# Decoding in one stage by sequence in a one-core hybrid decoder step: heads times tokens as stationary rows, pages sorted ahead

## The chip, the cores and the metric

The kernel runs on one core of a Trainium2 chip. All data are float32. The metric is the device time of one launch in microseconds (us); the time before is the median of 3 runs.

## The reference, cut to what matters

One layer of a decoder with three groups of heads that work side by side, run for a prompt of 4096 tokens and for a decode batch of 8 sequences with 8 new tokens each. The change touches only the decode part. For each sequence it computes:

```python
# A: window attention, 6 query heads over 2 key heads, 1024 cached + 8 new keys
oa = mix_dilations([dilated_sample(aq, ka, va, d, w // d) for w, d in ((128,1), (512,4), (2048,16))])
# B: sparse attention: an indexer with 8 heads picks 256 of the 1032 keys per query
kb, vb, ki = (concat(pool[page_table], new) for pool, new in ...)   # 8 pages of 128 rows per sequence
dots  = einsum('nthd,nsd->ntsh', iq, ki)
score = einsum('ntsh,nth->nts', relu(dots), iw)                     # weighted sum over the 8 heads
sel   = top_k(where(causal, score, -inf), 256)
ob    = softmax(bq @ kb[sel]) @ vb[sel]                             # 6 query heads over 2 key heads
# C: cross attention, 4 heads, 256 memory tokens per sequence
oc = softmax(cq @ mk) @ mv
y  = x + [silu(ag)*oa | silu(bg)*ob | silu(cg)*oc] @ w_out, then RMSNorm
```

A head has 64 dimensions. The three dilation patterns are one attention with a bias per distance (the logarithm of how many patterns hold a key). The pages of a sequence lie scattered in a pool of 80 pages.

## The kernel before, in words

The program is a row of stages, each with its own tiles and a barrier at its end: `project_memory`, `project_tokens`, `attend_window`, `attend_sparse`, then `attend_sampled` twice ("b" with heads B, and "a" with heads A and C), then `project_out`. A stage can't load anything before the one ahead is over. Intermediate results pass between stages through scratch tensors in HBM.

`attend_sampled` has two parts. The first (lines 1910 to 2040) is a loop over the 8 sequences with one buffer: SyncE and ScalarE issue the loads of a sequence, TensorE turns (transposes) its key blocks, VectorE copies them from PSUM to `kT`. The next sequence's loads wait until the last one's keys are turned (line 1962). For "b" each page is looked up in a register (line 1923), and its rows are loaded with their own DMAs: 64 for the keys, 64 for the values, 128 for the indexer keys.

The second part is `attend` (lines 547 to 1012), a general attention over row tiles. It holds all 64 queries (8 sequences times 8 tokens) of one head as the stationary operand, and since each sequence has its own keys, it does one product per sequence, with a stationary operand `qm` that is zero in all columns but that sequence's 8 (`scores`, line 687: 8 products accumulate into one bank). The weighted values work in the same way: `PT` holds for each key block 8 copies, each zero but for one sequence, so that a block of 128 keys takes 8 products of 64 columns (`values`, line 705). Indexer scores come first (8 heads times 3 chunks of 512, 512 and 128 columns, times 8 sequences), then VectorE adds up relu(score) times weight (lines 877 and 881), then it searches the cut for 256 keys per row by 12 rounds of halving (`rounds`, line 904, each one compare-and-count over 1152 columns and two short operations), asks TensorE whether some row needs 12 more rounds (line 742), picks the exact value among the 8 largest below, and makes the bias. Then the 6 heads of B follow, and in the next stage the 4 heads of C and the 6 of A.

`attend_sparse` (from line 1300) does the same for the prompt: 32 query tiles t, with SyncE's program (lines 1461 to 1489) in order: constants, first keys and queries, and then for each t it waits, loads the queries of tile t+4 and t+2 and stores the result of tile t-1. The engines wait for the constants at lines 1545 and 1841.

A float32 product shows as two matmul records, a transpose as one.

Of the kernel before, what the change touches and what calls it, by code (L numbers as in the profile page):

```python
# [23 lines left out]
F32 = mybir.dt.float32  # L24
BF16 = mybir.dt.bfloat16
U16 = mybir.dt.uint16
I32 = mybir.dt.int32
# [441 lines left out]
class Tally:  # L469

    def __init__(self, sem, credit, per, tiles):
        self.sem, self.credit, self.per = sem, credit, per
        self.base = [credit + sum(p * n for p, n in zip(per[:g], tiles[:g])) for g in range(len(per))]

    def at(self, g, j, k):

        if isinstance(j, int):
            return self.base[g] + j * self.per[g] + k  # L480
        return j * self.per[g] + (self.base[g] + k)


class Attend:


    def __init__(self, kind, head, chunks):
        self.kind, self.head, self.chunks = kind, head, chunks
        if kind == "C":
            self.slot, self.half, self.out = T_CQ + head // 2, head % 2, (12 + head) * HD  # L490
        else:
            self.slot, self.half = (T_AQ if kind == "A" else T_BQ) + head % 3, head // 3
            self.out = (head if kind == "A" else 6 + head) * HD


def spans(lo, hi):
    return [(c, min(512, hi - c)) for c in range(lo, hi, 512)]


STAGES = 6  # L500


class Group:

    def __init__(self, tiles, idx, b_chunks, a_chunks, kinds):
        self.tiles, self.idx = tiles, idx
        self.width = sum(w for _, w in idx)  # L510
        order = (0, 3, 1, 4, 2, 5)
        self.heads = []
        if "B" in kinds:
            self.heads += [Attend("B", h, b_chunks) for h in order]
        self.n_b = len(self.heads)
        a_heads = [Attend("A", h, a_chunks) for h in order] if "A" in kinds else []
        c_heads = [Attend("C", h, [(0, MEM)]) for h in range(4)] if "C" in kinds else []

        self.heads += c_heads + a_heads
        self.n_idx = 8 * len(idx)  # L520
        self.first = [0]
        for a in self.heads:
            self.first.append(self.first[-1] + len(a.chunks))
        self.n_att = self.first[-1]
        self.s_all = self.n_idx + self.n_att

        self.n_a = max([self.first[i + 1] for i, a in enumerate(self.heads) if a.kind == "A"], default=0)
        self.s_b = self.n_idx + self.first[self.n_b]


        self.tail = max(self.n_b, len(self.heads) - STAGES)

    def part(self, a, lo, hi, n):

        at = lambda k: n * (self.first[k] - self.first[lo]) // (self.first[hi] - self.first[lo])
        return (at(a), at(a + 1)) if lo <= a < hi else (0, 0)

FEW_ROUNDS, ROUNDS = 12, 24
ASKED = 6 + 3 * FEW_ROUNDS + 4
MORE = 1 + 3 * (ROUNDS - FEW_ROUNDS) + 4
LINKS = ASKED + 2 + MORE + 14


def attend(nc, tag, R, nseq, groups, io):

    tiles = [g.tiles for g in groups]
    W = max([g.width for g in groups] + [512])
    WB = max([sum(w for _, w in a.chunks) for g in groups for a in g.heads if a.kind == "B"] + [W])
    SW = max(sum(w for _, w in a.chunks) for g in groups for a in g.heads)
    topk = any(a.kind == "B" for g in groups for a in g.heads)
    lastw = io["causal_width"]
    ptw = R if nseq == 1 else nseq * (R // nseq * (nseq + 1))  # L560
    with ExitStack() as ctx:
        def sb(name, shape, dt=F32):
            return ctx.enter_context(nc.sbuf_tensor(f"{tag}_{name}", shape, dt))

        def tally(name, credit, per):
            each = [per(g) for g in groups]
            used = any(each)
            return Tally(ctx.enter_context(nc.semaphore(f"{tag}_{name}")) if used else None, credit, each, tiles)

        io["open"](ctx, sb)  # L570
        ident, q_sb = io["ident"], io["q"]
        S = sb("S", [R, 2, SW])
        PT = sb("PT", [P, 2, 4, ptw])
        o_sb = sb("o", [R, D])
        mc = sb("mc", [R, 2, 8])
        mjunk = sb("mjunk", [R, 2, 8])
        negm = sb("negm", [R, 2])
        lsum = sb("lsum", [R, 2])
        linv = sb("linv", [R, 2])
        zero_bias = sb("zero_bias", [R, MEM])  # L580
        if topk:
            X = sb("X", [R, W])
            relu = sb("relu", [R, 4, 512])
            Y = sb("Y", [R, W])
            GE = Y[:, :].bitcast(BF16)[:, 0:W]
            GT = Y[:, :].bitcast(BF16)[:, W:2 * W]
            rank = sb("rank", [R, W], U16)
            biasB = sb("biasB", [R, WB], BF16)
            col = sb("col", [R, 24])
            undone = sb("undone", [1, 1], I32)  # L590
# [41 lines left out]
        def wait(eng, t, g, j, k):  # L632
            eng.wait_ge(t.sem, t.at(g, j, k))
# [1789 lines left out]
```

## Time and profile before

| | us |
|---|---|
| median of 3 runs (range) | 7368.91 (7368.54 to 7378.87) |
| the profiled execution's own time | 7375.32 |
| its span, first to last instruction | 7373.6 |
| stage "b" of the decode, first SyncE issue to that of "a" | 6026.81 to 6512.15 |
| stage "a", to the first issue of `project_out` | 6512.15 to 6794.17 |

Over the whole span TensorE is busy for 85%, VectorE for 49%, ScalarE for 38%. Read these as an average over seven stages with different limits; the stages of the decode are read by their own stretches.

### The profile page before, as it was taken

How to read it: one execution, taken by the hardware profiler on the slowest of the kernel's cores; microseconds unless marked ns; L12 is line 12 of the kernel's file. 1: busy time of each engine (PE TensorE's matmuls, PEld its weight loads, DVE VectorE, ACT ScalarE, POOL GpSimd, SP SyncE). 2: the span in 40 equal slices, each digit the busy share in tenths (PEclk: the TensorE clock that was granted, in tenths of full speed). 3: DMA queues.
4: the chain of work that ended last, by engine and by line, in shares of the span. 5: the costliest groups of instructions: out<-in, count | busy, mean ns of one | idle time of the engine just before them, and what ended most of it. 6: DMA issues, size and time to landing. Idle time of an engine off the chain costs nothing. (4 is left out here: it accounts for less than half of the span.)

```text
span 7373.6 us, 83535 instructions
## 1 busy us (share of the span) xinstructions
PE 6301.1 (85%) x27915; PEld 3737.0 (51%) x27915; DVE 3636.7 (49%) x9459; ACT 2834.3 (38%) x5992; POOL 113.6 (2%) x179
## 2 busy tenths in 40 slices
PE   6999999998999867888888888888888864858898
PEld 3444444445667634555555555555555642445444
DVE  1111111113555568888877777776776611210554
ACT  1222222223545534555555555555555520000232
POOL 0000000000000100000000000000000000000000
PEclk8999999999999978999999999999999977979999
DMA  3111111115000030000000000000000011021443
GB/s 116 51 44 47 49 51 48 42 45 140 30 26 34 29 85 16 16 11 11 11 11 6 6 11 6 6 6 6 6 7 1 4 26 48 1 74 49 141 150 129
DMA packets 261720, 294.02 MB, mean 40 GB/s; under 512 B 57700, under 2 KB 226660, under 8 KB 260196
## 3 DMA queue, kind: packets, MB, share of 16 engines
q1 hardware_dynamic: 226196, 240.36, 10.3%
q0 software_dynamic: 12368, 40.71, 1.5%
q10 hardware_dynamic: 22784, 8.40, 0.4%
q8 instruction: 184, 3.01, 0.2%
q14 instruction: 188, 1.54, 0.1%
HBM read 181.88 MB, written 109.60 MB: 40 GB/s over the span
## 5 line engine op out<-in xcount | busy, mean ns | idle before, releaser
L453 PE MATMUL t_zp<-t_w,t_xT 128*128 128x512 f32 (+1 forms) x3696 | 1443.1, 551 | 42.5 <-DVE t_w L406 42.5
L1514 PE MATMUL p_SC<-p_ikT,p_iq 128*128 128x512 f32 (+3 forms) x2272 | 1119.0, 599 | 217.2 <-DVE p_mc L1654 216.9
L1541 PEld LDWEIGHTS p_OP<-p_bv,p_PT 128*128 128x128 f32 x6336 | 877.6, 202 | 587.9 <-ACT p_PT L1580 284.6
L453 PEld LDWEIGHTS t_zp<-t_w,t_xT 128*128 128x128 f32 x3696 | 662.5, 192 | 778.3 <-issue 735.5
L1589 ACT ACTIVATE p_relu<-p_SC 128x512 f32<-128x512 f32 (+3 forms) x1136 | 633.5, 565 | 1076.1 <-PE p_SC L1514 954.6
L1541 PE MATMUL p_OP<-p_bv,p_PT 128*128 128x64 f32 x6336 | 872.8, 282 | 148.8 <-ACT p_PT L1580 148.6
L1505 PE MATMUL p_SC<-p_bkT,p_bq 128*128 128x512 f32 (+3 forms) x1728 | 884.9, 595 | 32.0 <-DVE p_mc L1654 31.8
L1514 PEld LDWEIGHTS p_SC<-p_ikT,p_iq 128*128 128x128 f32 x2272 | 440.6, 202 | 783.2 <-issue 422.8
L1654 DVE CUSTOM_DVE_ANT_0 p_S<-p_SC,p_bias 128x512 f32<-128x512 f32 (+3 forms) x864 | 554.5, 645 | 407.4 <-PE p_SC L1505 335.8
L1687 DVE SCALAR_TENSOR_TENSOR p_X<-p_relu,p_iw,p_X 128x1024 f32<-128x1024 f32 (+7 forms) x546 | 608.4, 1114 | 220.0 <-ACT p_relu L1589 213.1
L1580 ACT ACTIVATE p_PT<-p_TP 128x512 f32<-128x512 f32 (+3 forms) x864 | 481.4, 557 | 445.7 <-PE p_TP L1531 444.4
L288 ACT ACTIVATE t_z<-t_zp,t_rstd 128x512 f32<-128x512 f32 (+1 forms) x231 | 146.7, 635 | 1310.9 <-PE t_zp L453 1310.9
L1531 PE MATMUL p_TP<-p_ident,p_S 128*128 128x128 f32 x3168 | 533.1, 290 | 103.1 <-ACT p_S L1572 102.5
L1721 DVE TENSOR_SCALAR_CACHE_REDUCE p_Y<-p_X,p_col 128x384 bf16<-128x384 f32 (+29 forms) x240 | 609.6, 2540 | 1.0 <-issue 0.3
L1256 ACT ACTIVATE w_S<-w_S,w_o 128x256 f32<-128x256 f32 (+1 forms) x704 | 339.0, 482 | 416.0 <-DVE w_o L1222 416.0
L1572 ACT ACTIVATE p_S<-p_S,p_negm 128x1024 f32<-128x1024 f32 (+7 forms) x480 | 476.3, 992 | 16.8 <-DVE p_mjunk L1660 16.8
L1531 PEld LDWEIGHTS p_TP<-p_ident,p_S 128*128 128x128 f32 x3168 | 406.7, 164 | 126.0 <-ACT p_S L1572 120.5
L2305 PE MATMUL f_zp<-f_w,f_mixT 128*128 128x512 f32 x1056 | 463.9, 598 | 0.0
L1231 DVE COPY w_PT<-w_TP 128x512 f32<-128x512 f32 (+1 forms) x352 | 226.7, 644 | 263.3 <-PE w_TP L1166 263.0
L1184 PEld LDWEIGHTS w_OP<-w_v,w_PT 128*128 128x128 f32 x2052 | 250.6, 191 | 158.5 <-DVE w_PT L1231 158.5
L2305 PEld LDWEIGHTS f_zp<-f_w,f_mixT 128*128 128x128 f32 x1056 | 200.8, 193 | 240.6 <-issue 240.6
L1184 PE MATMUL w_OP<-w_v,w_PT 128*128 128x64 f32 x2052 | 290.1, 282 | 21.2 <-DVE w_PT L1231 20.7
(247 smaller groups left out, 5559.5 us busy)
## 6 DMA issues: line engine op xcount, KB each, us to landing
scr_qkT<-t_qT SPq DMA_DIRECT2D x33, 960.0 KB, 3.7
scr_part<-w_o POOLq DMA_DIRECT2D x96, 198.0 KB, 2.2
f_part<-scr_part SPq DMA_DIRECT2D x32, 594.0 KB, 4.8
t_x<-in_x_prompt SPq DMA_DIRECT2D x32, 512.0 KB, 3.6
f_gate<-scr_gate SPq DMA_DIRECT2D x32, 512.0 KB, 7.2
f_x<-in_x_prompt SPq DMA_DIRECT2D x32, 512.0 KB, 3.7
out_y_p<-f_y POOLq DMA_DIRECT2D x32, 512.0 KB, 6.5
p_iq<-scr_qkT SPq DMA_DIRECT2D x120, 128.0 KB, 2.9
```

The costliest lines, as they stand in the source:

```text
L453: mm = pe.matmul(zp[(NZ * p + c) % 2][:, 0:n], xT[:, p, k, :], w[:, k, a:a + n], start=(k == 0), stop=(k == KD - 1))
L1184: mm = pe.matmul(OP[u % 2][:, h, :], PT[:, k % 2, 2 * b + s, :], val, start=(b == U.blocks[0]), stop=(b == 1))
L1505: pe.matmul(bank(ring["B", n, g])[:, 0:w], bq[:, t % 2, n % HEADS, :], bkT[:, 512 * g:512 * g + w], start=True, stop=True).then_inc(s_read ...
L1514: pe.matmul(bank(ring["I", t, k])[:, 0:w], iq[:, t % 2, h, :], ikT[:, 512 * c:512 * c + w], start=True, stop=True).then_inc(s_ready, 1)
L1531: mm = pe.transpose(TP[m % 2][:, b, :], S[:, n % 3, c0:c0 + P], ident[:, :])
L1541: mm = pe.matmul(OP[n % 2][:, 0:HD], PT[:, m % 2, b, :], bv[:, 4 * g + b, s * HD:(s + 1) * HD], start=(g == 0 and b == 0), stop=(last and ...
L1580: act.activation(PT[:, m % 2, 0:nb, :], TP[m % 2][:, 0:nb, :], ACT.Copy).then_inc(pT_ready, 1)
L1589: act.activation(relu[:, j % 3, 512 * (c % 2):512 * (c % 2) + w], SC[r % 4][:, 0:w], ACT.Relu, scale=0.5)\
L1654: dve.tensor_tensor_reduce(S[:, n % 3, cols], SC[r % 4][:, 0:w], bias[:, cols], -SCALE, -FAR, ALU.add, ALU.min, mc[:, p, g:g + 1]).then_in ...
L1687: dve.scalar_tensor_tensor(x, r, w, x, ALU.mult, ALU.add).then_inc(idx_added, 1)
L1721: link(dve.tensor_scalar(G[:, 0:L], X[:, t % 2, 0:L], c(W + 1), None, ALU.is_gt, ALU.add, accum_out=c(CNT)))
L2305: mm = pe.matmul(zp[2 * p + i][:, :], mixT[:, p, k * P:(k + 1) * P], w[:, k, i * 512:(i + 1) * 512], start=(k == 0), stop=(k == KD - 1))
```

## The change

The two decode stages and `attend` with its helpers go; one new `attend_sampled` takes their place. It has these parts:

- **Pages.** `attend_sparse` now also copies the pages of all sequences in order into scratch tensors, HBM to HBM, with SyncE's DMAs: 24 per tile t for t = 4 to 11. It loads the page table with its constants (one more DMA before the first keys).
- **Keys.** A sequence's keys, values and indexer keys are loaded with one DMA each, 8 consecutive rows per partition, so that key order in `kT` is "partition within block" (host tables `window_s` and the bias follow that order). Keys and values of A and B share the tiles `kn` and `v`, with room for all 8 sequences.
- **Indexer.** Per sequence: 8 turns, then one product each for 512, 512 and 8 keys, with 8 heads times 8 tokens as the 64 stationary columns; relu on ScalarE; then 3 products with `pick_w` (the indexer weights, laid out so that they add up the heads of each token) that accumulate over the sequences in 3 banks.
- **Attention.** 24 units: C, A and B for each of 8 sequences. The stationary operand has 48 columns (6 heads times 8 tokens; half of each column zero, by key head) or 32 for C. The bias is added by a product with a selection matrix `sel` (for B it reads `bias` in steps of 8 elements). Values are one product per key block, 128 columns wide (256 for C), computed for both key heads. Scores stay in PSUM; ScalarE's exp reads them there.
- **Search.** 24 rounds always, 2 after each of units 1 to 12, over 1032 columns; the ends of the search after units 13, 14 and 15. The check on TensorE goes.
- **Output.** 16 small DMAs (6 heads of A, 6 of B, 4 of C).

The diff, cut to its core:

```diff
@@ attend_sparse
+            def sort_pages(n):
+                for b in range(PAGES):
+                    page = sp.value_load(table[0:1, n * PAGES + b:n * PAGES + b + 1], min_val=0, ...)
+                    for name, to in (("cache_idx_k", "page_i"), ("cache_dsa_k", "page_k"), ("cache_dsa_v", "page_v")):
+                        sp.dma_start(scr[to][n * PAST + b * PAGE:n * PAST + (b + 1) * PAGE, :],
+                                     ins[name][bass.ds(page * PAGE, PAGE), :]).then_inc(const_in, 16)
+            sp.dma_start(table[:, :], ins["page_table"]).then_inc(const_in, 16)
             keys(0)
...
                 if t:
                     store(t - 1)
+                if 4 <= t < 4 + NSEQ:
+                    sp.wait_ge(const_in, 128)
+                    sort_pages(t - 4)
...
@@ attend_sampled (new), SyncE
+            sp.dma_start(ident[:, :], ins["ident"]).then_inc(idx_in, 16)
+            for s in range(2):
+                sp.dma_start(iq[:, s:8:2, :], new_slots(slice(s * HD, (s + 1) * HD), T_IQ, T_AQ)).then_inc(idx_in, 16)
...
+            for h in range(8):
+                sp.dma_start(iw[h * TDEC:(h + 1) * TDEC, :], scr["iw"][SEQ:SEQ + R, h:h + 1]...).then_inc(idx_in, 16)
+            for n in range(NSEQ):
+                sp.dma_start(ikn[:, n, :, :], by_partition(scr["page_i"], n, PAGES)).then_inc(i_in[n], 16)
...
+            for n in range(NSEQ):
+                u = units.index(("A", n))
+                sp.wait_ge(turned, turn_at["K", u, 1] + 1)
+                sp.dma_start(kn[:, n, :, :], by_partition(scr["page_k"], n, PAGES)).then_inc(k_in[n], 16)
+                sp.wait_ge(v_done, u + 1)
+                sp.dma_start(v[:, n, :, :], by_partition(scr["page_v"], n, PAGES)).then_inc(v_in[n], 16)
+            for kind, done in (("C", 8), ("A", 16), ("B", 24)):
+                sp.wait_ge(o_out, done)
+                for head in range(4 if kind == "C" else 6):
+                    store(kind, TDEC * head, HD * (head if kind == "C" else head // 3), head)
@@ TensorE
+            def index(n):
...
+                    pe.matmul(score_bank(("I", n, c))[0:R, 0:w], iqn[:, n, :], keys, start=True, stop=True)
+            def sum_heads(n):
...
+                    pe.matmul(OP[c][0:R, 0:w], pick_w[:, n, :], relu[:, n % 2, a:a + w],
+                              start=(n == 0), stop=(n == NSEQ - 1)).then_inc(i_summed, 1)
+            def scores(u):
...
+                if kind == "B":
+                    pe.wait_ge(bias_ready, 1)
+                for c, (a, w) in enumerate(chunks(u)):
...
+                    to = score_bank((u, c))[0:rows, 0:w]
+                    pe.matmul(to, (qa if kind == "A" else qb)[:, n, :], keys, start=True, stop=False)
...
+                        add = bias[:, 0:PAST].rearrange("q (p b) -> q b p", b=PAGES)[:, 4 * c:4 * c + 4, :]
+                        to = to.rearrange("q (b p) -> q b p", p=P)
+                    pe.matmul(to, sel[:, n, :], add, start=False, stop=True).then_inc(s_ready, 1)
...
+            for n in range(NSEQ + 1):
+                if n < NSEQ: turn_index(n)
+                if n >= 1: index(n - 1)
+                if n >= 2: sum_heads(n - 2)
...
+            for u in range(NU + 2):
+                if u + 1 < NU: turn_keys(u + 1)
+                if u < NU: scores(u)
+                if 1 <= u <= NU: turn_probs(u - 1)
+                if u >= 2: values(u - 2)
@@ VectorE
+            for u in range(NU + 1):
+                if u + 1 < NU: keys(u + 1)
+                if u < NU: maxima(u)
+                if u >= 1: inverse(u - 1)
+                part(u)
@@ build
-    attend_sampled(nc, ins, outs, scr, "b", "B")
-    attend_sampled(nc, ins, outs, scr, "a", "AC")
+    attend_sampled(nc, ins, outs, scr)
```

The scores have 3 banks in turn (`score_bank` waits for the relu or exp that read the bank 3 uses ago), the turns have 2 (`turn_bank`).

## Rows read from the trace of the kernel before

**Rows 1.** Windows by stretch: us, busy us (instructions) per engine, clock, DMA share, GB/s.
```profile
6053.00:6196.00 143.00, 28.99 (x128) 26.00 (x128) 22.04 (x32) 0.00 (x0) 2.13 (x2) 0.55 0.30 77
6196.00:6324.00 128.00, 125.84 (x383) 49.44 (x384) 13.71 (x23) 11.36 (x23) 2.06 (x1) 0.98 0.00 1
6324.00:6368.00 44.00, 14.80 (x32) 4.53 (x31) 39.47 (x83) 0.27 (x1) 0.00 (x0) 0.65 0.00 0
6368.00:6509.00 141.00, 138.75 (x1179) 88.05 (x1178) 11.55 (x54) 13.80 (x35) 0.00 (x0) 1.00 0.00 1
...
6527.00:6610.00 83.00, 22.51 (x96) 19.38 (x96) 16.60 (x24) 0.00 (x0) 3.80 (x2) 0.54 0.48 136
6610.00:6791.00 181.00, 175.99 (x1406) 109.77 (x1406) 14.23 (x74) 18.13 (x52) 0.39 (x1) 0.99 0.00 1
```
**Rows 2.** Timeline (start us, us, what) at both ends of the decode.
```profile
6026.81 0.34 SPq L1976 DMA_DIRECT2D bk_ident<-in_ident  x1
...
6790.84 0.31 ACT L805 ACTIVATE a_o<-a_OP,a_linv 64x64 f32<-64x64 f32 x1 [4.33 <-PE a_OP L717]
...
6794.17 0.36 SPq L2125 DMA_DIRECT2D f_ident<-in_ident  x1
```
**Rows 3.** Groups by shape, TensorE, decode stages: busy us, mean ns.
```profile
L689 PE MATMUL b_SC<-bk_kT,bk_qm 128*64 128x512 f32 x448 | 198.9, 604 | 6.7 <-POOL b_PT L659 6.7
L717 PE MATMUL a_OP<-ak_v,a_PT 128*64 128x64 f32 x992 | 61.0, 222 | 4.3 <-ACT a_PT L794 4.3
L689 PE MATMUL a_SC<-ak_kT,ak_qm 128*64 128x128 f32 x96 | 11.5, 273 | 0.0
```
**Rows 4.** Timeline and chain, TensorE runs without a gap.
```profile
6628.97 3.62 PE L689 MATMUL a_SC<-ak_kT,ak_qm 128*64 128x256 f32 x16
...
7332.26 0.87 PE f_tp L2294 x8
7333.14 27.48 PE f_zp L2305 x64
```
**Rows 5.** Timeline, `attend_window`: keys read in steps (first), side by side (second).
```profile
1989.45 1.28 PE L1155 MATMUL w_SC<-w_akT,w_aq 64*128 64x256 f32 x4
...
2450.97 0.70 PE L1155 MATMUL w_SC<-w_ckT,w_cq 64*128 64x256 f32 x4
```
**Rows 6.** Groups by shape, VectorE and ScalarE, decode stages.
```profile
L2039 DVE COPY bk_kT<-bk_tr 128x512 f32 x32 | 22.0, 691 | 128.3 <-PE bk_tr L2015 127.0
L843 DVE CUSTOM_DVE_ANT_0 a_S<-a_SC,ak_biasA 64x512 f32<-64x512 f32 x12 | 8.2, 683 | 120.2 <-PE a_SC L689 120.2
L843 DVE CUSTOM_DVE_ANT_0 a_S<-a_SC,a_zero_bias 64x256 f32<-64x256 f32 x4 | 1.7, 416 | 26.1 <-PE a_SC L689 23.4 <-issue 2.7
L966 DVE TENSOR_TENSOR_SCAN b_rank<-b_Y 64x1152 uint16<-64x1152 bf16 x1 | 2.5, 2550 | 0.0
L848 DVE TENSOR_SCALAR_CACHE_REDUCE a_mjunk<-a_mc 64x3 f32<-64x3 f32 x6 | 0.9, 148 | 0.2
```
**Rows 7.** Timeline, VectorE: one round of the search and the next one's start.
```profile
6328.91 1.41 DVE L907 TENSOR_SCALAR_CACHE_REDUCE b_Y<-b_X,b_col 64x1152 bf16<-64x1152 f32 x1
...
6330.78 1.40 DVE L907 TENSOR_SCALAR_CACHE_REDUCE b_Y<-b_X,b_col 64x1152 bf16<-64x1152 f32 x1
```
**Rows 8.** DMA issues by line: count, KB each, median us to landing.
```profile
p_iq<-scr_qkT SPq DMA_DIRECT2D x120, 128.0 KB, 2.9
...
ak_nat<-in_cache_mem_k ACTq DMA_DIRECT2D x8, 256.0 KB, 4.4
```
**Rows 9.** Timeline of SyncE's issues in `attend_sparse`: one slow issue, tile 4, tile 12.
```profile
2582.91 6.49 SPq L1454 DMA_DIRECT2D p_bv<-out_dsa_v  x1
...
2798.60 2.60 SPq L1436 DMA_DIRECT2D p_iq<-scr_qkT  x4
2801.24 0.60 SPq L1439 DMA_DIRECT2D p_iw<-scr_iw  x1
...
3356.18 3.20 SPq L1436 DMA_DIRECT2D p_iq<-scr_qkT  x4
```

More of the change, by code:

```diff
@@ L466, in _ @@
             turn_z(NLAST, 0)
[L469 to L493, printed above, removed]
@@ L496, in spans @@
[L496 to L536, printed above, removed]
@@ L1857, in _, with attend_sampled, chunks, key_turns @@
                         all_seen()
-def attend_sampled(nc, ins, outs, scr, tag, kinds):
-    R, KEYS = NDEC, PAST + P
-    NB = KEYS // P
-    paged = kinds == "B"
-    keys = spans(0, KEYS)
-    groups = [Group(1, keys, [], [], ""), Group(1, [], keys, [], "B")] if paged else [Group(1, [], [], keys, kinds)]
-    DIAG = NSEQ * (R // NSEQ * (NSEQ + 1))
+def attend_sampled(nc, ins, outs, scr):
+    R, NEW = NDEC, PAST
+    KEYS = PAST + TDEC
+    L = KEYS
+    ROWS = {"A": 48, "B": 48, "C": 32}
+    units = [(kind, n) for kind in "CAB" for n in range(NSEQ)]
+    NU = len(units)
+    def chunks(u):
+        return [(0, 512), (512, 512), (NEW, TDEC)] if units[u][0] != "C" else [(0, MEM)]
+    def key_turns(u):
+        return 2 if units[u][0] != "C" else 1
+    first_chunk, first_turn = [0], [0]
+    for u in range(NU):
+        first_chunk.append(first_chunk[-1] + len(chunks(u)))
+        first_turn.append(first_turn[-1] + key_turns(u))
+    turn_at, turn_users, score_at, score_users = {}, [], {}, []
+    def plan_turn(name, user):
+        turn_at[name] = len(turn_users)
+        turn_users.append(user)
+    def plan_score(name, user):
+        score_at[name] = len(score_users)
+        score_users.append(user)
+    def plan_key_turns(u):
+        for i in range(key_turns(u)):
+            plan_turn(("K", u, i), ("keys", 2 * NSEQ + first_turn[u] + i + 1))
+    for n in range(NSEQ + 1):
+        if n < NSEQ:
+            for i in range(2):
+                plan_turn(("I", n, i), ("keys", 2 * n + i + 1))
+        if n >= 1:
+            for c in range(3):
+                plan_score(("I", n - 1, c), ("relu", 3 * (n - 1) + c + 1))
+    plan_key_turns(0)
+    for u in range(NU + 2):
+        if u + 1 < NU:
+            plan_key_turns(u + 1)
+        if u < NU:
+            for c in range(len(chunks(u))):
+                plan_score((u, c), ("exp", first_chunk[u] + c + 1))
+        if 1 <= u <= NU:
+            plan_turn(("P", u - 1), ("probs", u))
```

932 lines of the change are left out of this document (370 added, 562 removed).

## The prediction

> **What bounds the kernel now.** I read the windows first, stretch by stretch, since shares over the whole span mix seven stages. They show the decode in four kinds of stretch [rows 1]: two loops that load and turn keys, where TensorE is busy for 28.99 of 143 us and 22.51 of 83 us; two stretches of scores and values where it is busy nearly all the time (138.75 of 141 us, 175.99 of 181 us) at full clock; the indexer, 125.84 of 128 us; and the search, where VectorE is busy for 39.47 of 44 us and TensorE mostly waits. Nothing of these lies beside another. The timeline gives the ends: first issue at 6026.81 us, first issue of the output stage at 6794.17 us [rows 2]. So the decode costs **767.4 us**, a tenth of the span, and it is all path. The groups by shape say why the full stretches are long: 448 records of 512 columns for 64 stationary columns, 56 of which are zero, and 992 records of 64 columns for values [rows 3]. Eight products do what one could.
>
> **Prices.** One 512-column record takes 27.48 / 64 = 0.429 us in an unbroken run, a turn of 128 columns 0.87 / 8 = 0.109, a 256-column record 3.62 / 16 = 0.226 [rows 4]; a record of 128 columns 11.5 / 96 = 0.120, one of 64 columns 61.0 / 992 = 0.0615 [rows 3]. A float32 product is two records. The new products differ in height and stationary width (48 instead of 64), not in what moves through, so I use these.
>
> **Head of the new stage.** SyncE issues 13 DMAs before the first indexer keys: 5 at about 0.4 to 0.6 us and 8 small ones, 7 us at 0.60 each for the latter [rows 9]. Then 256 KB land in 4.4 us [rows 8]. The eight DMAs for the weights move single elements; I give them the same landing. TensorE starts 11.5 us in; no memset stands ahead of it. Bounds 9 and 20.
>
> **Indexer.** Per sequence 8 turns (0.87), 8 records of 512 columns (3.43), 4 of 8 columns (at most 0.25): 4.55 us, times 8 is 36.4. VectorE's two copies (2 x 0.69 [rows 6]) and ScalarE's relus, about as long, lie beside it, since the program turns one sequence ahead and sums one behind. TensorE comes out of a pause at the lower of its two clock levels: the load loops ran at 0.55 [rows 1]. With that and the last relu and sum: 3.5 us more. Then VectorE takes the three sums from PSUM and copies the first keys while TensorE waits: 3 us.
>
> **C units: VectorE sets the pace.** TensorE needs 4 turns (0.44), 4 records of 256 columns for scores and 4 for values (0.226 each, 1.81) and 2 small turns (0.22): 2.5 us. VectorE needs a copy (0.69), a maximum over 256 columns (0.42, the row of that size), three short operations with their read-outs (0.6, from 0.148 each [rows 6]), 0.2 for links, and two rounds. A round is 6330.78 - 6328.91 = 1.87 us [rows 7]; its long operation shrinks from 1152 to 1032 columns, 1.41 x 0.104 = 0.15 less: 1.72, two are 3.45. Together 5.35 us, times 8 is 43 us. This is where the search goes: before it stood alone.
>
> **A units: nearly level.** TensorE: 8 turns 0.87, scores 8 records of 512 (3.43) and 4 tiny ones (0.25), 9 turns of the probabilities at no more than 0.109 (0.98), 18 value records of 128 columns (2.16): 7.7 us, times 8 is 61.5. VectorE: two copies 1.38, two maxima at 0.68 [rows 6], a small one, short operations 0.9, two rounds 3.45: 7.2 us. So TensorE leads by 0.5 us in the first five. The last three units carry the ends of the search. The old stretch of the search is 44 us, less 12 x 1.87 leaves 21.6 for setting up, the question to TensorE, and the ends [rows 1, 7], among them a scan of 2.55 us [rows 6]; I put the ends at 15 us, 5 each, 1.6 over two rounds. Less the slack and plus the wait of the first B unit for its bias: 4 us. The bank ring also makes each unit's scores wait for the last one's exp: maximum, negation, exp, about 2.3 us from 0.68, 0.148 and an exp of a chunk; between them TensorE has probabilities, values and the next turns, 4.0 us, to do. Hidden, as long as VectorE answers at once.
>
> **B units.** The same 7.7 us, but the bias product reads every 8th element. The window stage shows such a read: four records of 256 columns with keys in steps take 1.28 us, against 0.70 side by side [rows 5], twice the time once the end of the run is taken off. Of the four records pairs run beside each other there, so the ratio is what carries over: four bias records of 0.429 gain between 0 (if only the queries' steps cost) and 1.72 us. I take 1.6: 9.3 us, times 8 is 74.4. VectorE (3.7) lies beside.
>
> **Clock, against the rule.** In the search TensorE was busy for 14.80 of 44 us and was granted 0.65; in dense stretches 0.98 to 1.00 [rows 1]. C units have it busy for 2.5 of 5.35 us, so I expect a clock below 1. At 1.2 GHz its 2.5 become 4.9 us, still under VectorE's 5.35: nothing lost. The first A unit can pay up to 7.7 us; I take 2. The Trainium skill (TensorE: Matmul & The Clock Gate, "HAM oscillation — how this bites in real kernels") says that a loop whose products are shorter than its waits starts each turn at half rate; by that rule the loss would return in every C unit, and the sum would be the same, since VectorE covers it.
>
> **Tail.** After the last values one output, six stores at about 0.5 us, of which the last lands 2 us later, and the next stage; before, the same way took 6794.17 - 6790.84 = 3.3 us [rows 2]. With the last wait for the exp: 6.5 us. The stores of C and A go out earlier.
>
> **Loads.** 7 MB must be in before the first A unit, 97 us into the stage, at 136 GB/s 51 us; all of A is 14 MB, 103 us, and the last A unit comes at 150 [rows 1]. B's loads of sequence n go out during A's unit n, 60 us ahead. Hidden. If the rate were 70 GB/s, A's units would wait some 50 us.
>
> **Sorting.** 24 issues and 8 look-ups in each of 8 tiles. At 0.60 us an issue [rows 9] and up to 1 us a look-up, 22 us. Tiles 4 to 11 last 3356.18 - 2798.60 = 557.6 us, 70 each, of which SyncE used 5. Behind the copies in SyncE's order stand the queries of two tiles ahead and the store of a tile with two buffers; both have more slack than 22 us. Traffic of 20 MB in 558 us is 36 GB/s beside nearly nothing. I take 0, bounds -1 and +30. The table's DMA ahead of the first keys delays the sparse stage by 0.6 to 1 us: 1.
>
> **Sum.** 11.5 + 36.4 + 3.5 + 3 + 43 + 61.5 + 4 + 2 + 74.4 + 6.5 = 246 us in place of 767.4: 521 less, plus 1. From the profiled execution's 7375.3 us that gives 6855. It stands 6.4 us over the median, so the **prediction is 6848 us**.
>
> **Rivals.** (1) *The two engines wait for each other in turn* (0.30). VectorE's margin in A is 0.5 us, the turns have 2 banks and the scores 3, so a late copy stops TensorE and then a late score stops VectorE. With A at 10, B at 10.5 and C at 6.5 us a unit this costs 18 + 10 + 9 = 37 us: 6885. For it speaks that maxima read PSUM in an order fixed by the program; against it the old stages, where TensorE's waits for the other two engines were small. (2) *Steps cost nothing and the seams are short* (0.15): the bias read is as fast as a plain one (-13) and head and tail are 5 us shorter: 6830. Against it stands the row of the window stage. (3) *The sorting goes wrong and eats it all* (0.02): slower than before. An issue that meets a full queue took 6.49 us [rows 9]. Of the 558 us of the eight tiles some 512 are free for SyncE, and the gain is 521, so it needs (512 + 521) / 192 = 5.4 us for each copy before the kernel is slower. At 6.49 the eight tiles take 1246 + 46 us in place of 558, and the kernel 6848 + 734 = 7580. Against it: between the tiles the queue is empty, and issues there take 0.60. (4) *The small DMAs or the loads hold the stage* (0.08): single-element DMAs landing at 20 us, or 70 GB/s: 6875 to 6900. The forecast itself has 0.45.
>
> **Numbers.** A difference under 0.2% (15 us) can't be told from none. The likeliest case's own range is 6832 to 6866; with rivals 1 and 2 the range is 6822 to 6895. Faster than before by over 0.2%: 0.97; within 0.2%: 0.01; slower: 0.02.
>
> **What would show it.** Right: one decode stage of some 246 us; C units spaced by 5 to 6 us with VectorE busy all along and a clock under 1; A units spaced by 7.7 and B units by 9 to 9.5 with TensorE busy; bias records of B twice as long as those of A; tiles 4 to 11 of the sparse stage as long as before. Wrong: A units spaced by over 8.5 us with both engines idle in part; B as short as A; a first turn later than 20 us; TensorE waiting for `kn` or `v`; the sparse stage longer by more than 5 us.

## The result, and the profile after

The changed kernel takes 6868.76 us (median of 4 runs, 6855.58 to 6893.19); the kernel before 7370.95 (median of 4, 7368.54 to 7378.87). The ratio is 0.932, with a 95% interval of 0.929 to 0.935. The forecast was 6848, the range 6822 to 6895. Two things want explaining: a median 21 us above the forecast, and runs 38 us apart where those of before lie within 10.

The profiled execution took 6855.58 us, the forecast's 6855 for that execution. That the two agree to a microsecond is luck: the decode took 4.6 us more than forecast, and all the rest of this execution (6605.0 us, before 6608.0) 4.0 us less than the 6609.0 that the forecast implies. Windows of the changed kernel, in the columns of [rows 1]: the sparse stage, then the decode in five stretches (head, indexer, C units, A units with the first B unit, B units; the limits lie near the changes from one kind of unit to the next, not on them).

```profile
2573.00:6017.00 3444.00, 2922.75 (x13588) 1865.75 (x13588) 2521.71 (x6135) 1841.62 (x3392) 1.59 (x2) 0.93 0.05 15
6017.00:6028.00 11.00, 2.39 (x11) 1.68 (x12) 2.18 (x4) 0.00 (x0) 3.01 (x5) 0.50 0.52 149
6028.00:6072.00 44.00, 41.68 (x173) 18.67 (x171) 15.89 (x34) 10.50 (x26) 0.00 (x0) 0.97 0.91 323
6072.00:6120.00 48.00, 35.37 (x130) 14.49 (x130) 42.42 (x133) 9.03 (x35) 0.00 (x0) 0.86 0.04 12
6120.00:6189.00 69.00, 65.32 (x356) 34.83 (x356) 49.30 (x135) 19.50 (x64) 0.00 (x0) 0.93 0.28 92
6189.00:6264.00 75.00, 74.31 (x358) 34.63 (x358) 20.52 (x71) 18.33 (x59) 0.00 (x0) 0.98 0.08 24
```

Before, three stretches had TensorE busy for a fifth to a third of the time, beside VectorE or beside transfers alone. Now TensorE is busy nearly all along behind the head (2.39 of 11 us), and the one stretch where it isn't (35.37 of 48 us) is VectorE's (42.42). The loads for the C and A units fall under the indexer, at 323 GB/s, so the 70 GB/s at which the A units would have waited was never near.

The timeline gives the ends, as in [rows 2]:

```profile
6016.79 0.34 SPq L1451 DMA_DIRECT2D d_ident<-in_ident  x1
...
6263.73 2.02 SPq L1448 DMA_DIRECT2D scr_o<-d_oB  x6
6267.39 0.36 SPq L1874 DMA_DIRECT2D f_ident<-in_ident  x1
```

The decode lasts 6267.39 - 6016.79 = **250.6 us** (before 767.4, forecast 246). Each unit leaves one output copy on ScalarE, and the starts of these copies give the spacing of the units: mostly 5.0 us for C (the first six copies lie 4.97 to 5.89 us apart), 8.12 for A, 10.03 for B.

TensorE in the steady B unit, and its waits over the decode:

```profile
6198.94 1.06 PE L1558 MATMUL d_SC<-d_kT,d_qb 128*48 128x512 f32 x2
6199.93 2.01 PE L1566 MATMUL d_SC<-d_bias,d_sel 64*48 64x512 f32 x2
6201.87 1.06 PE L1558 MATMUL d_SC<-d_kT,d_qb 128*48 128x512 f32 x2
6202.86 2.01 PE L1566 MATMUL d_SC<-d_bias,d_sel 64*48 64x512 f32 x2
```

```profile
PE d_TR L1509 <- DMA d_ikn<-scr_page_i: 11.6, 1, 11.6
PE d_TR L1537 <- DVE d_kT L1694: 9.6, 6, 3.1
PE d_SC L1558 <- DVE d_bias L1782: 3.0, 1, 3.0
```

From start to start the stepped bias pair takes 6201.87 - 6199.93 = 1.94 us, the pair of queries and keys 0.99. The waits (total us, times, longest) are the head, the copies in the C units, and one of 3.0 us for the bias ahead of the first B unit. In the steady A units there are none: between 6130 and 6165 us TensorE was busy for 35.00 of 35.

Outside the decode: the sparse stage runs from 2573.32 to 6016.79, 3443.5 us (before 3448.5). The output stage takes 586.4 us in place of 579.4; over the twelve traces with the new decode it lay between 583.5 and 592.4, and it took 585.6 in `one`, which has the decode stages of before. So the change needn't be the cause of these 7 us; their cause is open. The stages differ from trace to trace without any edit of theirs: the sparse stage with the sorting in it took between 3439.9 and 3457.2 us in eleven traces.

### The profile page after: what moved, and what is told of

It is laid out like the page before. It is cut to its first block and busy times, and to the rows that moved or that the text cites. A ratio compares the mean times of both kernels' runs of the same rounds, so it can differ in the third digit from the quotient of the medians.

```text
span 6853.8 us, 78452 instructions
## 1 busy us (share of the span) xinstructions
PE 6011.2 (88%) x25717; PEld 3541.6 (52%) x25717; DVE 3647.1 (53%) x9535; ACT 2846.6 (42%) x6063; POOL 91.9 (1%) x172
## 5 line engine op out<-in xcount | busy, mean ns | idle before, releaser
L638 PEld LDWEIGHTS w_OP<-w_v,w_PT 128*128 128x128 f32 x2052 | 250.6, 191 | 158.6 <-DVE w_PT L685 158.6
L386 DVE COPY t_qT<-t_tp 128x512 f32<-128x512 f32 (+1 forms) x132 | 81.4, 654 | 447.7 <-PE t_tp L439 446.6
```

## Experiments

Decode lengths below run from the stage's first DMA issue to that of the output stage, in the one profiled execution of each run. All but `late` and `one` have the sorting in the sparse stage. `late`, `one` and `rounds12` were executed once; the times of the others are of 4 or 5 executions.

**same** and **same2**: the changed kernel, unedited.

> The changed kernel itself, once more, to see what its spread of 38 us over four runs (6855.58 to 6893.19, against 10 us of the kernel before) is made of, and as the base of its neighbours in this job. Theory 'the spread lies in the long stages' (they are 6603 of 6854 us and have granted TensorE clocks of 0.91 to 0.99): the decode stage repeats within 2 us at 250.6, A units at 8.12 and B units at 10.03 us apart, the first B unit again near 16 us; differences lie in the projections, the sparse stage or the output stage, and go with their clock. Rival 'the new stage is unstable' (its engines wait for each other in turn, and the seam before the first B unit falls differently each time): the decode stage itself differs by over 10 us from 250.6.

> The changed kernel once more, beside the kernel with full products ahead of the indexer on one chip: the runs so far of the two were on different chips (4 for the latter, whose five runs lie within 5.7 us; 9 and another for the changed kernel, 38 and 43 us apart). Theory 'the indexer's clock stays low in some runs, and full products ahead of it prevent that': this kernel again has two groups of runs 34 us apart (two or three of six at 6885 to 6901), the other none. Rival 'it is the chip that differs': both kernels agree in their spread here.

`same`: 6858.08, 6862.28, 6895.10 and 6900.71; the decode of the profiled one 250.6 us, every spacing as before to 0.02 us. `same2`, on another chip: 6891.52 to 6901.45, all five, with a decode of 284.2 us. The 13 times of this kernel (4 of the result, 4 and 5 here) form two groups: five from 6855.6 to 6872.5, and eight from 6891.5 to 6901.5. Three of the 13 were profiled, two of the lower group and one of the higher. TensorE in one sequence of the indexer, in `same2`, and the window around it:

```profile
6059.47 3.67 PE L1518 MATMUL d_SC<-d_kT,d_iqn 64*64 64x512 f32 x4
...
6063.12 3.77 PE L1524 MATMUL d_OP<-d_relu,d_pick_w 64*64 64x512 f32 x6
6066.82 1.91 PE L1509 MATMUL d_TR<-d_ident,d_ikn 128*64 128x128 f32 x8
6068.66 3.67 PE L1518 MATMUL d_SC<-d_kT,d_iqn 64*64 64x512 f32 x4
```

```profile
6036.00:6056.00 20.00, 20.00 (x43) 7.51 (x42) 3.04 (x5) 3.73 (x9) 0.00 (x0) 0.50 1.07 340
6056.00:6076.00 20.00, 20.00 (x44) 7.53 (x42) 2.73 (x4) 2.49 (x6) 0.00 (x0) 0.50 0.83 333
6076.00:6096.00 20.00, 20.00 (x43) 7.50 (x43) 3.91 (x12) 2.49 (x6) 0.00 (x0) 0.50 0.00 0
```

and the same place in the first profile of the changed kernel:

```profile
6037.46 1.93 PE L1518 MATMUL d_SC<-d_kT,d_iqn 64*64 64x512 f32 x4
...
6039.31 1.97 PE L1524 MATMUL d_OP<-d_relu,d_pick_w 64*64 64x512 f32 x6
6041.22 1.06 PE L1509 MATMUL d_TR<-d_ident,d_ikn 128*64 128x128 f32 x8
6042.21 1.93 PE L1518 MATMUL d_SC<-d_kT,d_iqn 64*64 64x512 f32 x4
```

A sequence takes 9.19 us (6059.47 to 6068.66) instead of 4.75, with a granted clock of 0.50, the level of 1.2 GHz, from end to end although TensorE is busy every microsecond. The instructions are the same. The DMA share goes from 1.07 to 0.00 with no effect, so it isn't the loads. Both theories of `same` are half wrong: the stage is stable by unit, but the gap between the groups lies in it, in one place (284.2 - 250.6 = 33.6 us). Of the eight traces in which this indexer runs with nothing put ahead of it and its height unchanged, three (`after`, `same`, `early`) show it at 1.00 and five (`same2`, `plain`, `tall`, `rounds12`, `late`) at 0.50. That the unprofiled times of the higher group have the same cause is a conclusion from the times and from the clock of the whole execution, which is 0.939 to 0.942 in that group and 0.945 to 0.947 in the other.

**warm**: full products ahead of the indexer; **warm2**: the same beside `same2`.

```diff
+            pool.memset(warm[:, :], 1.0).then_inc(zeroed, 1)
...
+            pe.wait_ge(zeroed, 1)
+            for k in range(5):
+                pe.matmul(OP[2][:, :], warm[:, 0:P], warm[:, :], start=True, stop=True)
             pe.wait_ge(idx_in, IDX_IN)
```

> Five float32 products of 128 rows x 128 columns x 512 columns, on a tile of ones and into a bank that is written anew later, on TensorE while it would wait for the first indexer keys. The result is the same. Of six traces of kernels with this indexer, four show it at full clock (35 us at 1.00, first turn to first turn of the compressed units 40 us) and two at 0.50 from end to end (74.3 us), with the same instructions and TensorE busy all along; both the kernel's fast and its slow runs lie 34 us apart for that. Theory 'the products of 64 rows and 64 columns can't bring the clock up by themselves, but keep it': with full products ahead of them all runs have the indexer at 1.00, the high group of runs (6893 to 6901) is gone, the spread falls from 38 us to that of the kernel before (10 us), the median is 6855 to 6860 and the head of the stage is 0 to 2 us longer or shorter. Rival 'the low level is independent of what ran just before' (chance of the chip): 1 to 3 of 6 runs are still 34 us longer.

> The kernel with five full products ahead of the indexer once more, on the chip of its neighbour. Theory: all runs within 10 us of each other and of 6861. Rival 'it is the chip': its runs spread as its neighbour's do; with one run above 6885 the theory that the products prevent the low level falls.

(The first of these miscounts, and so does that of `high` below: until then three traces had shown the full clock and two the low one, and 3 of 8 times of the unedited kernel had been above 6885.) `warm`: 6861.57 (6859.23 to 6864.90, 5 runs). `warm2`: 6862.99 (6859.49 to 6870.74, 5 runs) where `same2`, on the same chip, has 6894.37. Ratios to before are 0.9315 (0.9302 to 0.9327) for `warm2` and 0.9358 (0.9345 to 0.9371) for `same2`. So five products whose result nobody uses save 31 us on that chip, and it isn't the chip that differs. Windows of `warm`:

```profile
6024.00:6028.00 4.00, 4.00 (x7) 1.58 (x6) 0.31 (x1) 0.00 (x0) 0.34 (x2) 0.59 0.34 56
6028.00:6036.00 8.00, 7.08 (x36) 3.50 (x35) 4.55 (x8) 1.49 (x4) 0.00 (x0) 1.00 1.06 306
6036.00:6060.00 24.00, 24.00 (x102) 10.97 (x101) 7.00 (x15) 6.39 (x16) 0.00 (x0) 1.00 1.04 361
```

The added products run from 6021.11 to 6028.7 us; the clock rises under them and stays up through the small ones. No run has five small products in their place, so that they must be full ones is not shown.

**high**: 128 rows for the indexer's scores.

```diff
-iqn = sb("iqn", [HD, NSEQ, R])
+iqn = sb("iqn", [P, NSEQ, R])      # rows 64 to 127 zero, as in kT
-  kT[0:HD, n % 2, 512 * c:512 * c + 512]
+  kT[:, n % 2, 512 * c:512 * c + 512]
```

> The indexer's scores (32 of its 48 long records and more, not its sums over heads) get 128 rows in place of 64, the lower half zeros; nothing is added ahead. The result is the same and the number of records too. Theory 'how much of the array a product uses decides whether the clock rises': no run with the indexer at 0.50, or fewer than before (2 of 6 traces, 4 of 9 times of the unchanged kernel above 6885), the median near 6858. In turn the switch of height in each sequence (128-row scores, 64-row sums) costs, by the 0.13 us seen in the A units, 2 x 0.13 us a sequence, 2 us in all. Rival 'only the number of records or the time busy counts': as many runs at 6893 as without, median 6875.

6866.90 (6863.67 to 6873.14, 5 runs), none in the group above 6885, no product added, decode 250.6 us. The edit gives 128 rows to 32 of the indexer's 64 long records (not of 48, as the expectation has it). With twice the rows under the same 64 columns the profiled run has the indexer at 1.00, and the other four times leave no room for 34 us more. The indexer itself, first turn to last sum, is 1.3 us longer than in `same`, where 2 were expected for the changes of height. That speaks for the theory, and against the rival; but only five runs on one chip stand behind it, and the unedited kernel was not run on that chip. The one run there with the old indexer in its old form is `late`, whose trace has it at 0.50.

**plain**: the bias put into key order once.

```diff
-    add = bias[:, 0:PAST].rearrange("q (p b) -> q b p", b=PAGES)[:, 4*c:4*c+4, :]
+    add = biasp[:, a:a + w]
...
-    link(dve.tensor_scalar(bias[:, :], bias[:, :], 1.0, -NEG, ...))
+    dve.tensor_scalar(biasp[:, 0:PAST].rearrange("q (b p) -> q p b", p=P),
+                      bias[:, 0:PAST].rearrange("q (p b) -> q p b", b=PAGES), 1.0, -NEG, ...)
```

> The bias of the B units is put into key order once, by the last VectorE operation of the search, and read side by side by TensorE. Theory 'the stepped read costs all that B is longer than A' (my term of 1.6 us a unit; the record takes 1093 ns for two where the window's takes 608): B units fall from 10.03 to 8.1 us apart, 8 x 1.9 = 15 us less, the decode stage at 236 to 238 us, less what a stepped VectorE operation over 1024 columns costs in front of the first B unit (1.07 us for 512 columns against 0.69, so about 1 us more). Rival 'B is longer for another reason' (its product with the queries, the values, or the clock after the seam): B stays above 9.5 us and the bias records keep their 1.0 us.

B units are 8.12 us apart, the same as A's. The bias pair in `plain`, 0.99 us from start to start:

```profile
6257.66 1.06 PE L1564 MATMUL d_SC<-d_biasp,d_sel 64*48 64x512 f32 x2
6258.65 1.06 PE L1559 MATMUL d_SC<-d_kT,d_qb 128*48 128x512 f32 x2
```

The read in steps was the whole difference, 1.91 us a unit, as the first theory has it. The decode took 271.9 us with the indexer at the low clock; less the 33.6 by which `same2` is longer than `same`, 238.3, an estimate. Its median, 6880.93 (6873.12 to 6894.40), can't show 12 us beside a clock that is worth 34.

**tall**: selector, window and bias with 128 rows.

```diff
-sel = sb("sel", [R, NSEQ, 48])
+sel = sb("sel", [P, NSEQ, 48])     # and window, bias; rows 64 to 127 zero
```

> The selector, the window and the bias get 128 rows instead of 64, with zeros in the lower half, so that all products of the A and B scores have the same height. The result is the same. An A unit takes 8.12 us and not the 7.7 that I summed, with TensorE busy all along; between a product of 128 rows and one of 64 the starts of two 512-column records lie 0.99 us apart, where 0.86 was expected; the indexer, where all have 64 rows, keeps 0.44 each. Theory 'changing the height costs some 0.13 us at each change': pairs return to 0.86 us, an A unit to 7.6 us (four pairs a unit, 0.5 us less), 8 x 0.5 = 4 us off A; in B, where the stepped record is 1.94 us a pair, up to as much again, 4 to 8 us in all. Rival 'the pair costs 0.99 whatever the height' (alternating weights, or two accumulations into one bank): no unit moves by over 0.1 us.

A units are 7.51 us apart, B units 9.47. An A unit in the first profile of the changed kernel, then the same place in `tall`:

```profile
6164.74 1.06 PE L1558 MATMUL d_SC<-d_kT,d_qa 128*48 128x512 f32 x2
6165.73 1.06 PE L1566 MATMUL d_SC<-d_window,d_sel 64*48 64x512 f32 x2
6166.72 1.06 PE L1558 MATMUL d_SC<-d_kT,d_qa 128*48 128x512 f32 x2
```

```profile
6170.95 1.02 PE L1569 MATMUL d_SC<-d_window,d_sel 128*48 128x512 f32 x2
6171.80 1.02 PE L1561 MATMUL d_SC<-d_kT,d_qa 128*48 128x512 f32 x2
6172.66 1.02 PE L1569 MATMUL d_SC<-d_window,d_sel 128*48 128x512 f32 x2
```

The pair is back at 0.86 us; each change between 128 and 64 rows had cost 0.13. More zeros to multiply, less time. The decode is 272.7 us, 239.1 after taking off the low clock's 33.6: some 11.5 less, where 4 to 8 were expected; 2 of it lie at the first B unit, where the clock's fall is shorter here (3.4 us in place of 10.2). The median, 6878.80 (6842.39 to 6891.94), shows this no better than that of `plain`.

**early**: the ends of the search one unit sooner.

```diff
-                elif u <= 12:
-                    rounds(2 * u - 2, 2 * u)
-                elif u < 16:
-                    (mask_above, pick_value, make_bias)[u - 13]()
+                elif u <= 11:
+                    extra = max(0, min(2, u - 8))
+                    rounds(2 * u - 2 + max(0, min(2, u - 9)), 2 * u + extra)
+                elif u < 15:
+                    (mask_above, pick_value, make_bias)[u - 12]()
```

> The last four of the 24 rounds are done two at a time earlier (three rounds instead of two in the units 9 and 10), and the three ends of the search one unit sooner, so that the bias is ready a unit before TensorE wants it. Now the first B unit waits 3.02 us for it, after which the granted clock is 0.54 and the unit takes 16.05 us instead of 10.03. Theory 'the wait brings the clock down, and the clock costs the other 3 us': both go, the first B unit takes 10 to 10.5 us, the decode stage is 6 us shorter (244.6), less up to 0.3 us in each of the two units with three rounds, where VectorE (28 of 35 us busy) then needs 8.3 us. Rival 'the clock falls for another reason at that place' (the stepped bias, or chance): the 3 us of waiting go, but the unit still takes 13 us and the granted clock is under 0.8. Second rival 'three rounds overrun': units 9 and 10 take over 9 us and give back what the seam saves.

The wait for the bias is gone, and the first B unit takes 11.45 us in place of 16.05; the decode is 247.3 us, 3.3 less. The clock still falls, but later and for a shorter time (3.4 us in place of 10.2). Windows of `early` around the first B unit:

```profile
6174.00:6178.00 4.00, 3.77 (x12) 0.77 (x9) 1.38 (x2) 0.66 (x2) 0.00 (x0) 1.00 0.83 265
6178.00:6182.00 4.00, 4.00 (x18) 1.36 (x17) 1.55 (x6) 0.00 (x0) 0.00 (x0) 0.94 0.00 1
6182.00:6186.00 4.00, 4.00 (x24) 3.60 (x23) 0.30 (x5) 2.37 (x8) 0.00 (x0) 0.63 0.00 0
```

So the 3 us of waiting are not the clock's only reason; neither theory holds alone. The two A units with three rounds take 8.34 us, 0.2 more, and the last interval before the first B unit takes 8.74, 0.6 more; so 4.6 us saved become 3.3. The median, 6890.16 (6851.01 to 6894.10), has four of five runs in the group of the low clock and can't show them.

**rounds12**: one round a unit, `rounds(u - 1, u)`; the output is another.

> The search does one round a unit in place of two, so 12 of its 24 rounds are left out and the selected keys may be others. Theory 'VectorE sets the pace of the compressed units and TensorE that of the A units': the C units, now 5.02 us apart, come 1.72 us closer (3.3 to 3.5 us), or down to 4.9 us only where TensorE is then at its lower clock level; the A units stay at 8.12 us to 0.05. In all 12 to 14 us off the stage at full clock. Rival 'the engines wait for each other in turn': the A units get shorter too, by 0.3 us or more, since 28 of 35 us on VectorE become 19.

C units, by the output copies on ScalarE:

```profile
6126.51 0.45 ACT L1655 ACTIVATE d_oC<-d_OP,d_linv 32x256 f32<-32x256 f32 x1
6129.81 0.45 ACT L1655 ACTIVATE d_oC<-d_OP,d_linv 32x256 f32<-32x256 f32 x1
6133.10 0.45 ACT L1655 ACTIVATE d_oC<-d_OP,d_linv 32x256 f32<-32x256 f32 x1
```

3.30 us apart, one round (1.72) less than 5.02, and the A units stay at 8.12. VectorE sets the pace of the one, TensorE of the other; the engines don't wait for each other in turn. The decode is 274.2 us with the indexer at the low clock, 10.0 less than in `same2` and not the expected 12 to 14: the first B unit, with its fall of the clock, takes 1.1 us more than there, and one B unit 1.6 more.

**late**: the sorting at the head of the decode stage, the loop over `sort_pages(n)` moved out of the sparse stage and waited for.

> The sorting of the pages into scratch is moved from the sparse stage to the head of the decode stage, where nothing covers it: the page numbers are fetched, 8 x 24 copies issued, and the first load waits for the last of them. The work is the same. Theory 'the sorting is hidden in the sparse stage, and what it costs in the open is SyncE's issue time': blocks of three copies 2.57 us apart, 64 of them, 165 us, plus the fetch and the last landing (3 + 3 us): decode stage 250.6 + 171 = 421 us, the sparse stage as long as now (3443.5 us), time 7027. Rival 'in the open the copies are bound by their own traffic' (20 MB read and written): at the 140 GB/s of the first loads it takes 143 us for reading alone, 286 us for both ways, and the time is 7140; the issues then meet full queues. Second rival 'the sorting costs the sparse stage something now': it gets shorter by more than 3 us.

SyncE in `late`, the first copies, the last block, and what comes behind it:

```profile
6019.73 0.59 SPq L1446 DMA_DIRECT2D scr_page_i<-in_cache_idx_k  x1
...
6022.43 0.49 SPq L1446 DMA_DIRECT2D scr_page_i<-in_cache_idx_k  x1
...
6184.90 0.53 SPq L1446 DMA_DIRECT2D scr_page_v<-in_cache_dsa_v  x1
6187.11 0.36 SPq L1454 DMA_DIRECT2D d_ident<-in_ident  x1
```

The sorting takes 6187.11 - 6017.48 = 169.6 us in the open, at 2.6 us for a block of three (64 of them from 6019.73 to 6185.43). The sparse stage without it lasts 3443.65 us in this trace, with it 3443.5 in the first profile. That these two agree within 0.2 us is chance, since the same stage with the sorting differs by 17 us from trace to trace. The eight tiles alone are a narrower measure: from the issue of `p_iw` in tile 4 to that in tile 12 they take 553.4 to 560.3 us in the eleven traces with the sorting, and 554.2, 558.2 and 558.3 in the three without it (`late`, the kernel before, `one`). So a piece of work worth 170 us, a third of the gain, costs nothing that can be seen beside a variation of 7 us. The second rival's 3 us can't be told apart from this variation. The decode is 203 us longer than 250.6: the 170, and 34 for the indexer, which ran at the low clock in this profile; the time is 7064.41 us, the forecast 7027 plus these 34 and 3 more. The traffic of 20 MB held nothing up (the DMA share was 0.24 during the sorting), so the first rival falls.

**one**: the kernel before, `range(1)` for `range(nseq)` in its score and value loops.

> The kernel before, with the products of one sequence in place of all eight in its score and value loops of the decode (7/8 of these products are left out, the output of the decode is another). It splits the gain of 517 us. By the groups of before, 448 + 96 score records at 0.44 and 0.12 and 992 value records at 0.0615 are 272 us of start-to-start time, of which 7/8 go: 233 to 238 us. Theory 'TensorE bounds the full stretches (138.75 of 141 and 175.99 of 181 us)': the decode falls from 767.4 to 530 us, and the other 280 us of the change's gain come from doing loads, turns, search and attention beside each other. Rival 'behind TensorE another engine is close': the stretches are left with the copies, maxima and exps of VectorE and ScalarE (11.55 and 13.80 of 141 us, so not close) or with waits from one to the other, and the decode stays above 580 us.

7046.02 us, the decode 433.9: 333.5 less than before. My expectation was wrong in its input: it took three groups of the decode's products and there are more (192 further records of 512 columns, 864 further of values). All of them, at the prices of the prediction, are 640 x 0.429 + 64 x 0.226 + 320 x 0.12 + 1856 x 0.0615 = 442 us, 7/8 of that 386. Of the 53 us that didn't come, TensorE's group of long score records in `one` shows 34.9 as waits for VectorE, behind the search; what holds the other 18 is open (the group, then the window over the old indexer with 125.84 of 128 us in [rows 1], now with the search in it):

```profile
L689 PE MATMUL b_SC<-bk_kT,bk_qm 128*64 128x512 f32 x56 | 32.4, 719 | 41.6 <-DVE b_mc L843 34.9 <-POOL b_PT L659 6.7
```

```profile
6196.00:6324.00 128.00, 49.38 (x248) 24.57 (x246) 86.86 (x215) 24.94 (x60) 6.72 (x4) 0.66 0.02 5
```

So of 517 us some 333 come with not multiplying by zeros. The other 184 are what the rest of the change brings on top of it: the overlap of loads, turns, search and attention, one stage in place of two, fewer DMAs, pages sorted ahead. No run separates these. `one` is a single execution, and another order of the two steps could share the 517 us differently.

**best2**: plain, tall, early and warm together.

> The four edits together: bias in key order (B units 10.03 to 8.12 us apart, stage 12.8 us shorter when the indexer runs at full clock), selector, window and bias of 128 rows (A units 8.12 to 7.51, the stage 12 us shorter), the ends of the search a unit earlier (3.3 us shorter), and the full products ahead of the indexer. If they add up: A and B units both 7.5 us apart, the stage 250.6 - 12.8 - 12 - 3.3 = 222.5 us, less 2 to 3 because with both of the first two the B unit saves its height switch twice over or not at all (its bias pair was 1.94 and becomes 0.86). The time 6827 us with the indexer at full clock, and always there by the first theory of the run with products ahead; 6861 in a third of the runs by its rival. A rival for the sum: with A units of 7.5 us VectorE (28 of 35 us in five units of 7, or 7 us a unit, and 8.7 with three rounds) becomes the bound, and the units with three rounds take 8.7: 2.4 us back.

6834.40 us (6827.35 to 6840.69, 5 runs), ratio to before 0.928 (0.926 to 0.929), beside `warm` at 6861.57 on the same chip; the forecast was 6827. The decode is 221.5 us, the forecast 222.5 less 2 to 3. B units are 7.51 us apart, and so are the A units that VectorE doesn't hold up. The granted clock of the B units is 1.00 (this window goes to the end of the stage, so the tail's idle 4 us are in it):

```profile
6180.00:6246.00 66.00, 61.91 (x404) 39.65 (x402) 22.78 (x79) 20.07 (x67) 0.00 (x0) 1.00 0.13 38
```

The first B unit takes 7.49 us, with no fall of the clock. VectorE now does hold three of the A units (8.35, 8.35 and 9.44 us), as the rival for the sum has it for the first two; the third is the one beside the last end of the search, which no theory had.

## Why the prediction was right, and where it was off

The gain of the decode, 517 us of the 521 forecast, came by the way that the prediction describes: one product for eight, the search beside C and A units, the sorting under the sparse stage. The sizes below are mostly a few microseconds off, in both directions.

In the order of its sum, cut at events of the trace (first turn, end of the indexer, starts of the output copies), for the profiled run:

| piece | forecast us | measured us |
|---|---|---|
| head | 11.5 | 8.8 |
| indexer with clock ramp | 39.9 | 40.2 |
| transition, 8 C units, 2 A units, clock | 3 + 43 + 15.4 + 2 = 63.4 | 57.6 |
| 6 A units | 46.2 | 48.6 |
| first B unit with its wait | 9.3 + 4 = 13.3 | 16.1 |
| 7 B units | 65.1 | 70.3 |
| tail | 6.5 | 9.1 |
| sum | 245.9 | 250.6 |

- **Head.** The eight single-element DMAs took 2.95 us to issue, 0.37 each, not the 0.60 of [rows 9], and the first keys were there 2.9 us after their issue, not 4.4.
- **Indexer.** Right in this run. The term for its clock was mis-sized in others: 3.5 us in my sum; 34 more in eight of 13 times. I had asked what the clock does in the C units, where TensorE waits, and took a busy TensorE to be enough elsewhere. The runs show that it isn't: busy with products of 64 rows and 64 columns it can stay at the lower level. What decides between the two levels when nothing is put ahead is open.
- **The median's 21 us.** Only one of the result's four times, 6893.19, is of the low clock; without it the median is 6865.07. So the indexer's clock accounts for 3.7 of the 21 us. The decode, 250.6 us in place of 246, accounts for 4.6. The other 12 lie outside the decode as traced: the prediction takes 6.4 us off the profiled execution's time, since that of before stood so much over its median, while that of after was the fastest of 13. Runs with the indexer always at the full clock show the same (`warm` 6861.57, `warm2` 6862.99, decode 250.4 and 250.3: 14 and 15 us over the forecast with 4 of them in the decode). Which stage holds these 10 to 12 us is open.
- **C units.** VectorE's pace, as forecast and as `rounds12` shows; 5.02 rather than 5.35: what stands between two pairs of rounds takes 1.5 us (6078.57 to 6080.07), and I gave it 1.9. Over eight units that is 2.6 of the 5.8 us by which the row is shorter. The interval of the first A unit is 8.7 us, where I had 7.7 and 2 for the clock; that is 1 more. The lower clock in the C units (0.86) cost nothing.
- **A units.** The right engine, 0.4 us too short: the price of a record came from runs of equal height, and here heights alternate. Without the alternation (`tall`) the unit takes 7.51, so the other terms were 0.2 too long. Rival 1 needed TensorE idle; there is no such wait.
- **First B unit.** Mechanism right (it waits for its bias, 3.0 us), size short: the clock fell to 0.50 for 10.2 us from 6177.1 on, and the unit took 3 us more than the wait and a steady unit together.
- **B units.** The doubling of the stepped read was right, and `plain` gives all of it back: 1.91 us against 1.6. The other 0.4 of the 0.7 us by which a unit is longer (10.03 against 9.3) is the error of the A unit again. Rival 2 needed this read to be free.
- **Tail.** 3.1 and 2.0 us between the last three output copies, then 4.05 to the next stage; no run takes it apart.
- **Sorting.** 20.3 us of SyncE a tile (22 forecast), 0 on the clock as far as a variation of 7 us over the eight tiles lets see, and 170 in the open. Nothing came near the 5.4 us a copy of rival 3.
- **Rivals and range.** None of them is what moved the median; the 34 us were in no case of mine. On the chip of `same2` the median of the same kernel is 6894.37, inside the range by 0.6 us. That the range reached so far is luck: its upper end was made for rival 1.

The Trainium skill (TensorE: Matmul & The Clock Gate, "HAM oscillation — how this bites in real kernels"), by which a loop with waits longer than its products starts each turn at half rate, was weighed for the C units alone. The trace agrees in part: there the granted clock falls to 0.50 and returns to 1.00 four times, with every second unit and not with each; the mean is 0.86, with VectorE covering it, as either reading had it.

## What to carry to other kernels

When small products are packed densely, don't take a busy TensorE for one at full clock: read the granted clock of that stretch, and try a run with full products ahead or with zero rows added. If the repeated times fall in two groups, open a trace of each and compare the granted clock stretch by stretch. Price a record from rows with the same neighbours: alternating heights cost 0.13 us a change here, and a moving operand read in steps twice its time, so pad with zero rows and put a reused operand into order once, on an engine with time to spare. Work that one queue can do under another stage is worth its full time in the open, 170 us here, and a run with it moved into the open shows both sides at once; but hold the difference against how much the covering stage varies by itself (here 17 us over the stage, 7 over the tiles concerned). And a forecast for the median that is carried over from one profiled execution carries that execution's place among its times along.

## What the runs showed of the hardware that I had not expected

- TensorE busy for 73.99 of 74 us at a granted clock of 0.50 (`tall`, 6024 to 6098; products of 64 rows and 64 columns with turns between them). The same in five traces of eight, and by the times in 8 of 13 executions of the unedited kernel, on one chip five out of five; after five full products, or with 128 rows for half of the long records, in none of 15.
- 0.13 us for each change between products of 128 and 64 rows (0.99 us a pair against 0.86); none between products of one height.
- The same two records of 512 columns in 0.99 us side by side and 1.94 us with a step of 8 elements.
- With no wait ahead of it the first B unit still had its clock fall to 0.63 for some us (`early`), and not once the stepped read and the change of height were gone (`best2`). Which of the two it needs is open. With the wait left in, the fall to 0.50 lasted 10.2 us in the unedited kernel, 3.4 in `tall` (heights equal) and 13.7 in `plain` (no stepped read), so neither edit alone removes it.
